# Cross attention's scores as three fp32r passes over high and low halves

## The reference, cut to what matters

```python
hc = rmsnorm(x, norm_cross_g[l])
m = rmsnorm(mem, norm_mem_g[l])
qc = (hc @ w_q_cross[l]).reshape(B, S, CROSS_HEADS, CROSS_HEAD_DIM)
kvc = (m @ w_kv_cross[l]).reshape(B, M, 2, CROSS_HEADS, CROSS_HEAD_DIM)
sc = jnp.einsum('bshd,bmhd->bhsm', qc, kvc[:, :, 0]).astype(jnp.float32) * (CROSS_HEAD_DIM ** -0.5)
pc = jax.nn.softmax(sc, axis=-1).astype(x.dtype)
oc = jnp.einsum('bhsm,bmhd->bshd', pc, kvc[:, :, 1]).reshape(B, S, CROSS_HEADS * CROSS_HEAD_DIM)
x = x + oc @ w_o_cross[l]
```

## Time and profile before

| what | value |
|---|---|
| median of 3 runs | 1568.97 us (1568.84 to 1570.36) |
| the profiled execution | 1569.27 us, of which the span of its instructions 1567.4 us |
| PE busy | 1546.3 us, 99% of the span |
| DVE, ACT, POOL busy | 985.7, 790.6, 577.4 us |
| granted clock of PE, mean | 0.997 of full speed |

### The profile page before, as it was taken

The page is one execution under the profiler, slowest core; times in us unless marked ns, Lnnn a source line. Parts: engine busy times, 40 slices in busy tenths (PEclk is TensorE's granted clock), DMA queues, the critical chain, the costliest instruction groups (busy, mean ns, idle before and its releaser), DMA issues.

```text
span 1567.4 us, 20288 instructions
## 1 busy us (share of the span) xinstructions
PE 1546.3 (99%) x7624; PEld 1266.4 (81%) x7624; DVE 985.7 (63%) x1226; ACT 790.6 (50%) x926; POOL 577.4 (37%) x248
## 2 busy tenths in 40 slices
PE   9999999999999999999999999999999999999998
PEld 7888788887888888888889868767888888888886
DVE  6366231492465799999877489764554574656556
ACT  5265223434245788888865161694334453424344
POOL 1422363433442222322222836344332335252524
PEclk9999999999999999999999999999999999999999
DMA  5421242222237899999966324401420405050511
GB/s 207 128 74 54 84 146 86 81 81 80 85 109 296 322 421 417 385 387 391 385 269 232 113 84 135 122 1 58 158 81 29 160 27 188 28 188 27 176 53 54
DMA packets 49192, 250.89 MB, mean 160 GB/s; under 512 B 9888, under 2 KB 12704, under 8 KB 22880
## 3 DMA queue, kind: packets, MB, share of 16 engines
q1 hardware_dynamic: 42480, 236.59, 41.1%
q0 software_dynamic: 5184, 8.40, 1.5%
q10 hardware_dynamic: 1456, 4.92, 0.8%
HBM read 234.27 MB, written 16.78 MB: 160 GB/s over the span
## 4 chain that ended last, share of the span: by engine, by line
PE 83%; issue 6%; DVE 4%; POOL 4%; ACT 2%; DMA 1%; SPq 0%; ACTq 0%; POOLq 0%; DVEq 0%
PE psum L232 23%; PE psum L234 23%; PE psum L233 23%; POOL w_both L148 3%; PE psum L703 2%; PE psum L2466 2%; PE psum L2501 1%; PE psum L1437 1%; PE psum L2489 1%; PE psum L705 1%; ACT w_both L142 1%; PE psum L724 1%; PE psum L2790 1%; PE psum L2386 1%; PE psum L761 1%
## 5 line engine op out<-in xcount | busy, mean ns | idle before, releaser
L148 POOL TENSOR_TENSOR w_both<-raw,w_both 128x2048 fp32r<-128x2048 f32 x62 | 289.1, 4664 | 456.1 <-ACT w_both L142 421.1
L232 PE MATMUL psum<-x_hi,w_both 128*128 128x512 f32 (+1 forms) x624 | 243.6, 390 | 4.8 <-POOL w_both L148 4.8
L1455 DVE TENSOR_TENSOR moe_lo<-moe_w,moe_hi 128x2048 fp32r<-128x2048 f32 x100 | 228.3, 2292 | 31.4 <-ACT moe_hi L1445 30.2
L233 PE MATMUL psum<-x_lo,w_both 128*128 128x512 f32 (+1 forms) x624 | 240.8, 386 | 0.0
L234 PE MATMUL psum<-x_hi,w_both 128*128 128x512 f32 (+1 forms) x624 | 240.8, 386 | 0.0
L142 ACT ACTIVATE w_both<-raw 128x2048 fp32r<-128x2048 f32 x67 | 128.0, 1911 | 203.9 <-PE psum L234 201.9
L1445 ACT ACTIVATE moe_hi<-moe_w 128x2048 fp32r<-128x2048 f32 x100 | 191.5, 1916 | 27.9 <-PE psum L234 21.9
L2918 POOL TENSOR_TENSOR unit_lo<-mlp_raw,unit_hi 128x2048 fp32r<-128x2048 f32 x24 | 111.1, 4630 | 180.1 <-ACT unit_hi L2913 102.4
L232 PEld LDWEIGHTS psum<-x_hi,w_both 128*128 128x128 f32 x624 | 118.0, 189 | 30.6 <-issue 7.7
L233 PEld LDWEIGHTS psum<-x_lo,w_both 128*128 128x128 f32 x624 | 117.9, 189 | 23.5 <-issue 0.7
L234 PEld LDWEIGHTS psum<-x_hi,w_both 128*128 128x128 f32 x624 | 117.9, 189 | 23.5
(11 more groups left out here) (450 smaller groups left out, 3343.8 us busy)
## 6 DMA issues: line engine op xcount, KB each, us to landing
raw<-in_w_dense SPq DMA_DIRECT2D x67, 1024.0 KB, 4.9
moe_w<-in_w_moe_ahead SPq DMA_DIRECT2D x54, 1024.0 KB, 13.1
moe_w<-in_w_moe SPq DMA_DIRECT2D x48, 1024.0 KB, 12.7
mlp_raw<-in_w_mlp SPq DMA_DIRECT2D x28, 1024.0 KB, 4.9
yrow<-expert_rows SPq DMA_DIRECT2D x8, 512.0 KB, 7.2
res<-in_x SPq DMA_DIRECT2D x4, 512.0 KB, 6.5
hn_rows<-hn_tok ACTq DMA_DIRECT2D x4, 512.0 KB, 5.5
raw<-in_w_dense SPq DMA_DIRECT2D x2, 512.0 KB, 5.5
```

The lines of the kernel that those rows point to most:

```text
L148: pool.tensor_tensor(w_lo[c % RING][:, :], raw[c % RING][:, :], w_hi[c % RING][:, :].bitcast(F32), ALU.subtract).then_inc(lo_ready, 1)
L232: pe.matmul(out, lh, rh, start=first, stop=False, **more)
L233: pe.matmul(out, lh, rl, start=False, stop=False, **more)
L1455: dve.tensor_tensor(ring_lo[s][:, :], ring[s][:, :], ring_hi[s % MOE_HI][:, :].bitcast(F32), ALU.subtract).then_inc(moe_low, 1)
```

## The change

The scores are computed with `three_pass` instead of plain f32 matmuls. For it the keys get a high half `kc_hi` (ACT, `keys_high_part`) and a low half `kc_lo` (DVE, in the keys' own place), and each query tile a high half in `y_hi[:, j]` (ACT, `queries_high(j)`) and a low half in `y_lo[:, j]` (DVE, `queries_low(j)`). The queries' f32 tile `qc` shrinks from eight to four places, so `scaled(j)` for j of 4 and more waits for the low half of j - 4; the keys' high half lies where the other four places were. `scores(h)` waits for both low halves of its queries, and that of head 0 for the keys' low half. The new instructions stand on ACT in the hooks behind the splits of the chunks, on DVE between the ones that were there. Four semaphores of earlier stages are used again, counted from `BEFORE4`.

```diff
--- before.py
+++ after.py
@@ -2638,8 +2638,12 @@
 
     norm_cross = Norm("norm_cross", res, "cross", 144, hi=x_hi, lo=x_lo, bank=4, deferred=True)
     norm_mlp = Norm("norm_mlp", res, "mlp", 160, hi=x_hi, lo=x_lo, bank=4, rstd_kb=174, deferred=True)
-    qc = at("q_cross", 160, [P, KT, S])
+    qc = at("q_cross", 160, [P, 4, S])
     kc = at("k_cross", 176, [P, KT, MEM])
+    kc_hi = at("k_cross_hi", 168, [P, KT, MEM], FR)
+    kc_lo = at("k_cross_lo", 176, [P, KT, MEM], FR)
+    cq_high, cq_low, ck_high, ck_low = esq_done, esum_sq, y_split, xq_low
+    BEFORE4 = TB
     vc = at("v_cross", 184, [P, MEM // P, D])
     cs = [at(f"cross_score{b}", 144 + 4 * b, [P, TB, MEM]) for b in range(2)]
     ct_hi = [at(f"cross_prob_t_hi{b}", 152 + 4 * b, [P, MEM // P, S], FR) for b in range(2)]
@@ -2683,11 +2687,20 @@
                 ins = act.activation(cs[h % 2][:, q, :], cross_z[h % 2][:, 256 * q:256 * (q + 1)], ACT.Exp, bias=cnm[h % 2][:, q:q + 1], scale=CH_DIM ** -0.5,
                                      accum_out=csm[h % 2][:, q:q + 1])
             ins.then_inc(cs_exp, 1)
+        def queries_high(j):
+            act.wait_ge(bank_free, FIRST_TILE["q_cross"] + 4 + j + 1)
+            act.activation(y_hi[:, j, :], qc[:, j % 4, :], ACT.Copy).then_inc(cq_high, 1)
+
+        def keys_high_part():
+            act.wait_ge(kv_moved, 48)
+            act.activation(kc_hi[:, :, :], kc[:, :, :], ACT.Copy).then_inc(ck_high, 1)
+
         def values_high():
-            act.wait_ge(kv_moved, 48)
             act.activation(vc_hi[:, :, :], vc[:, :, :], ACT.Copy).then_inc(vc_high, 1)
-        dense_act(act, "q_cross", hooks={0: lambda: [norm_cross.act_root(act), values_high()], 1: lambda: exp(0),
-                                         2: lambda: exp(1)})
+        dense_act(act, "q_cross", hooks={
+            0: lambda: [norm_cross.act_root(act), keys_high_part(), queries_high(0), queries_high(1), values_high()],
+            1: lambda: [queries_high(2), queries_high(3), exp(0)],
+            2: lambda: [queries_high(4), queries_high(5), exp(1)], 3: lambda: [queries_high(6), queries_high(7)]})
 
         def copy_t(h):
             act.wait_ge(ct_done2, COUNTED + h + 1)
@@ -2718,7 +2731,13 @@
         def scaled(j):
             t = FIRST_TILE["q_cross"] + j
             dve.wait_ge(tile_done, t + 1)
-            dve.tensor_tensor(qc[:, j, :], psum[:, t % 4, :], norm_cross.rstd[:, :], ALU.mult).then_inc(bank_free, 1)
+            if j >= 4:
+                dve.wait_ge(cq_low, BEFORE4 + j - 3)
+            dve.tensor_tensor(qc[:, j % 4, :], psum[:, t % 4, :], norm_cross.rstd[:, :], ALU.mult).then_inc(bank_free, 1)
+
+        def queries_low(j):
+            dve.wait_ge(cq_high, BEFORE4 + j + 1)
+            dve.tensor_tensor(y_lo[:, j, :], qc[:, j % 4, :], y_hi[:, j, :].bitcast(F32), ALU.subtract).then_inc(cq_low, 1)
         add_residual(dve, "out2", norm_cross)
         norm_cross.wait_inverted(dve)
         dve.wait_ge(bank_free, FIRST_TILE["q_cross"] + 4)
@@ -2747,18 +2766,30 @@
             dve.wait_ge(cv_high, COUNTED + t + 1)
             dve.tensor_tensor(y_lo[:, t, :], psum[:, values_in(t // 2, t % 2), :], y_hi[:, t, :].bitcast(F32), ALU.subtract)\
                .then_inc(cv_low, 1)
-        for j in range(4):
-            scaled(j)
+        scaled(0)
+        scaled(1)
+        queries_low(0)
+        queries_low(1)
+        dve.wait_ge(ck_high, BEFORE4 + 1)
+        dve.tensor_tensor(kc_lo[:, :, :], kc[:, :, :], kc_hi[:, :, :].bitcast(F32), ALU.subtract).then_inc(ck_low, 1)
+        scaled(2)
+        scaled(3)
         dve.wait_ge(vc_high, AT_INDEX + 1)
         dve.tensor_tensor(vc_lo[:, :, :], vc[:, :, :], vc_hi[:, :, :].bitcast(F32), ALU.subtract).then_inc(vc_low, 1)
+        queries_low(2)
+        queries_low(3)
         top(0)
         scaled(4)
         normalise(0)
         scaled(5)
+        queries_low(4)
+        queries_low(5)
         top(1)
         scaled(6)
         normalise(1)
         scaled(7)
+        queries_low(6)
+        queries_low(7)
         turned_low(0)
         top(2)
         normalise(2)
@@ -2781,14 +2812,17 @@
         def scores(h):
             b = h % 2
             pe.wait_ge(bank_free, FIRST_TILE["q_cross"] + 4 + 2 * (h + 1))
+            pe.wait_ge(cq_low, BEFORE4 + 2 * h + 2)
             if h == 0:
-                pe.wait_ge(kv_moved, 48)
+                pe.wait_ge(ck_low, BEFORE4 + 1)
             if h >= 2:
                 pe.wait_ge(cs_exp, COUNTED + h - 1)
             for q in range(TB):
                 for half in range(2):
-                    mm = pe.matmul(cross_z[b][:, 256 * q:256 * (q + 1)], qc[:, 2 * h + half, q * P:(q + 1) * P],
-                                   kc[:, 2 * h + half, :], start=(half == 0 and q % 2 == 0), stop=(half == 1), skip_group_check=True)
+                    j, n = 2 * h + half, slice(q * P, (q + 1) * P)
+                    mm = three_pass(pe, cross_z[b][:, 256 * q:256 * (q + 1)], y_hi[:, j, n], y_lo[:, j, n],
+                                    kc_hi[:, j, :], kc_lo[:, j, :], half == 0 and q % 2 == 0, half == 1,
+                                    skip_group_check=True)
             mm.then_inc(cs_done, 1)
 
         def transposes(h):
```

## The result

The changed kernel is slower: 1576.24 us, median of 6 runs, against 1569.66 us for the kernel before in 6 runs; the recorded ratio is 1.0038, 95% interval 1.0027 to 1.0049 (the two medians alone give 1.0042). On the forecast's base of 1568.97 us that is 1574.9 us by the ratio and 1575.6 by the difference of the medians. Two repeats gave 1.0047 (1.0033 to 1.0061) and 1.0040 (1.0026 to 1.0054). The loss is 6 to 7 us where 4.4 were forecast.

The account below looks back on a forecast made before the run. PE bounds the kernel, with DVE and ACT's head-2 work bounding part of the stage. Savings of 0.57 x 3, waits of 1.6 and 4.7, and 0.15 given back make 1568.97 + 4.4 = 1573.4 us; range 1569.6 to 1575.8.

Parts of the forecast that it names:

- Scores on PE: Score matmuls: 24 fp32r matmuls per head, 0.120 us each, save 0.57 us a head, 2.28 us for four.
- First wait: At scores(0): PE waits for the keys' low half and loses 1.6 us.
- In between: Between scores(0) and values(0): POOL holds vc_lo and low 4 and 5, but all stays hidden, costing PE nothing.
- Second wait: At values(0): POOL's split holds low 6 and 7, turned_low(0) queues behind; PE stands 4.7 us, values(0) begins 4.6 later.
- the way to transposes(2): From values(0) to the third transposes: DVE's chain absorbs scores(3)'s saving; they start 4.45 us late.
- plus 0.25: On the way to the third transposes: copy_t(1) ends a little later than DVE wants it, adding 0.25 us.
- last sign: Forecast would be wrong if the third transposes didn't start about 4.4 us late.
- the likeliest case: POOL's split holds DVE's new subtractions near values(0); 1573.4 us, own range 1572.3 to 1574.8, chance 0.71.
- E: DVE's backlog meets another POOL split or delays o_cross: one more 2 to 3 us hold, 1575.5 to 1576.5; chance 0.11.
- B: New subtractions not held by POOL: PE waits 1.0 us at values(0), 1569.8 us in all; chance 0.10.
- C: Everything in the stage is hidden and PE keeps 4 x 0.57 us: 1566.7 us; chance 0.03.
- D: Part of the shift is given back later, as DVE and ACT fall better against POOL: 1570.5 to 1572; chance 0.05.

Follow-up runs that it names:

- e2: Changed kernel with POOL's split of the last q_cross chunk waiting for the queries' low halves 6 and 7; 1572.14 us, ratio 1.0018.
- e3: Changed kernel reordered: ACT makes queries high 6 and 7 behind copy_t(0), DVE low 6 and 7 behind turned_low(0) and top(2); 1569.55 us, 0.9999 of before.
- e1: The filler: changed kernel plus 20 thrown-away matmuls of 512 columns on PE between scores(2) and values(0); 1575.80 us, ratio 1.0040 to before.
- e7: e6 with POOL's split of the last q_cross chunk waiting for normalise(2); 1567.97 us, 0.9988 of before.
- e6: e3 with the keys' halves made in two parts, head 0's two key tiles first; 1568.12 us, 0.9990 of before.

## Why the prediction was right, and where it fell short

The direction and all terms of the sum but one held. **Scores on PE:** 24 matmuls in 2.88 us were forecast; 0.12 us apart they are, with 2.94 where the first starts from a standstill. **First wait:** 1.6 us forecast, 1.5 to 1.6 measured, released by the keys' low half as said. **In between:** hidden, as said; `vc_lo` was held (6.33 us), and low 4 and 5 (5.29), and no wait of PE came of them. **Second wait:** 4.7 forecast and measured; `values(0)` starts 48.13 us behind POOL's split of tile 1 (1172.96 less 1124.83) for 43.38 before (1167.08 less 1123.70), 4.75 later where 4.6 were forecast. e2 shows the hold as the cause of 3.7 us of it and leaves 1.0 to ACT's order, and e3 that the work in another order brings no wait there at all.

**The term that was mis-sized is the third, the way to transposes(2).** I took PE's own work from `values(0)` on to run at the pace it had before, "0.57 less", ending by 1178.8, so that DVE and ACT's chain would be the later one. But PE had stood still for 4.7 us, its granted clock fell to the lower level, and `values(0)` took 5.22, 4.83 and 5.10 us in the three profiles of the changed kernel, from its first matmul to the second transposes, where it takes 2.88 and 2.90 with the filler. So `transposes(1)`, and `copy_t(1)` behind them, came late, and PE's way became the later one. In the sum this is the "plus 0.25" that the prediction gave to a late `copy_t(1)`; DVE waited 2.69 us for it, and 0.35 in e1 with the clock kept up:

```profile
1180.37 1.29 DVE L2761 TENSOR_TENSOR cross_prob_t_lo<-psum,cross_prob_t_hi 128x512 fp32r<-128x512 f32 x2 [2.69 <-ACT cross_prob_t_hi L2710]
```

```profile
1177.63 1.29 DVE L2761 TENSOR_TENSOR cross_prob_t_lo<-psum,cross_prob_t_hi 128x512 fp32r<-128x512 f32 x2 [0.35 <-ACT cross_prob_t_hi L2710]
```

The forecast gave the third transposes 4.45 us late; with the clock kept up by the filler they are 55.84 - 51.05 = 4.8 late, without it 58.01 - 51.05 = 7.0. The missing term is thus 2.1 to 2.2 us, and 0.3 us are spread over the other hand-overs. The prediction had worked out the wait that made the clock fall, and didn't ask what the clock does in it. The trace of the kernel before could have told: behind its longest wait of PE the matmuls start 0.428 us apart (374.39 to 378.24 are nine of them), at a granted clock of 0.50:

```profile
373.81 0.79 PE L232 MATMUL psum<-x_hi,w_both 128*128 128x512 f32 x1 [3.60 <-POOL w_both L148]
374.39 0.63 PE L233 MATMUL psum<-x_lo,w_both 128*128 128x512 f32 x1
...
378.24 0.63 PE L233 MATMUL psum<-x_lo,w_both 128*128 128x512 f32 x1
```

By its own last sign, third transposes about 4.4 us late, the prediction failed: they came 7.0 us late in the stage. The time, too, lies above the range that the likeliest case gave itself (1572.3 to 1574.8). It lies within the whole range because that had been widened for E, which didn't happen, so this part is luck.

**The rivals.** B (no hold): its 1.0 us wait came only when e2 took POOL away, so it was the right price for a case that wasn't this one. C: keeping all of the 4 x 0.57 us needs more than moving low 6 and 7; even e7 wins only 1.7 us of stage time, as the way over DVE and ACT to the third transposes becomes the bound (0.9 us of waiting there). D (given back later): none; the time behind the stage is the same to 0.3 us in all kernels. E (one more hold, in `o_cross`): none; its time came near the measured one for another reason.

The Trainium skill's rule on the shared port (SBUF — State Buffer, "Who interferes with whom") held in both orders: the two-input operation that comes second is blocked until the first ends (the pair of 1166.48 took 5.23 for 1.29 us), and in e6 POOL was the second and took 5.37 for 4.61 us.

## What to carry to other kernels

A new elementwise operation with two SBUF inputs on DVE is to be priced with what POOL does at that moment, and by what is queued behind it: here 1.3 us of subtractions, with the copies on ACT that feed them, cost 4.7 us of PE, and the same instructions in another order left no wait at that place. When a forecast finds a wait of several microseconds on PE, the matmuls behind it have to be priced at the lower clock too (here 2.1 to 2.2 us on top of 4.7). In these traces that held behind waits of 3.6 and 4.7 us; behind waits of 1.0 to 2.4 us the full clock was right. Look for the first consumer of an operand that is prepared in one large piece: the keys of the first head in a piece of their own removed a wait of 1.6 us.

## What the runs showed of the hardware that was not expected

PE's granted clock fell to its lower level behind 4.7 us without a matmul (0.52 in the stretch of `values(0)`), and behind the wait of 3.6 us near 370 us, which every kernel has. It stayed at 1.00 behind waits of 1.0, 1.6 and 2.4 us (e2 and the changed kernel). How many matmuls then ran slowly was not the same in each execution: five to twelve behind the wait of 3.6 us. With 20 matmuls in place of the idle time it stayed at 1.00, and the kernel with more work was the faster one in the stage by 2.2 us.

That the tiny `cnmax` (128 x 4, one SBUF input and a constant) is held by POOL's split the prediction had read from the trace. New is how far it counts: it took 2.03 us in e2 and 1.05 in e3 against 0.17 in e7. So on this stage's path the smallest instruction can carry the wait to PE.
